# Turning the value product of an attention stage round, and scaling its output instead of its probabilities

## The reference

```python
def block(args):                       # one block of 128 queries of the fox attention
    i, q_b, cq_b = args
    s = jnp.einsum('bqhd,bkhd->bhqk', q_b, k, preferred_element_type=jnp.float32) * (d ** -0.5)
    s = s + cq_b[..., :, None] - ck[:, :, None, :]
    qpos = i * BLOCK_Q + jnp.arange(BLOCK_Q)
    s = jnp.where(kpos[None, :] <= qpos[:, None], s, NEG_INF)
    w = jax.nn.softmax(s, axis=-1).astype(v.dtype)
    return jnp.einsum('bhqk,bkhd->bqhd', w, v)
```

## Time and profile before

| | us |
|---|---|
| time, median of 3 runs | 2120.86 |
| lowest and highest of the 3 | 2119.37, 2122.98 |
| span of the profiled execution, its first to its last instruction | 2126.5 |
| first attention stage: first score product to first output-projection matmul | 134.2 to 243.1 |
| second attention stage, the same | 882.2 to 1015.6 |

### The profile page before, as it was taken

The page is one execution under the profiler, slowest core; times in us unless marked ns, Lnnn a source line. Parts: engine busy times, 40 slices in busy tenths (PEclk is TensorE's granted clock), DMA queues, the critical chain, the costliest instruction groups (busy, mean ns, idle before and its releaser), DMA issues.

```text
span 2126.5 us, 24646 instructions
## 1 busy us (share of the span) xinstructions
PE 1994.8 (94%) x9028; PEld 1647.9 (77%) x9028; DVE 915.8 (43%) x1321; ACT 317.2 (15%) x612; POOL 1240.5 (58%) x719
## 2 busy tenths in 40 slices
PE   7988889999997999999999999988898999999998
PEld 6767778888886787787778888876687778888886
DVE  2469464234338511278263253357537951000234
ACT  0036330000003100056110000020321121000001
POOL 4575356667775455633466667755454365666675
PEclk9989899999999899889999999999998999999999
DMA  5310123333232222211233333332221123333322
GB/s 202 119 40 1 55 72 115 95 99 99 93 95 93 68 88 89 70 35 45 80 100 98 99 96 92 98 109 67 74 81 59 48 82 93 95 99 99 93 95 79
DMA packets 53404, 181.23 MB, mean 85 GB/s; under 512 B 6552, under 2 KB 9290, under 8 KB 53210
## 3 DMA queue, kind: packets, MB, share of 16 engines
q1 hardware_dynamic: 46512, 165.17, 24.6%
q10 hardware_dynamic: 6826, 15.11, 2.1%
HBM read 176.56 MB, written 3.70 MB: 85 GB/s over the span
## 4 chain that ended last, share of the span: by engine, by line
PE 81%; DVE 12%; ACT 2%; issue 2%; POOL 2%; ACTq 0%; POOLq 0%; DVEq 0%
PE PS L577 78%; PE PS L721 2%; DVE PB L1252 1%; DVE X L1360 1%; PE PS L770 1%; DVE PTL L1258 1%; ACT PTH L1750 1%; DVE X L1361 1%; POOL WL L482 1%; DVE X L1322 1%; DVE STL L1594 1%; POOL WH L479 1%; DVE X L1422 0%; DVE XTL L1351 0%; DVE X L1305 0%
## 5 line engine op out<-in xcount | busy, mean ns | idle before, releaser
L479 POOL TENSOR_SCALAR WH<-RW 128x1024 fp32r<-128x1024 f32 x303 | 358.8, 1184 | 742.8 <-PE PS L577 706.1
L482 POOL TENSOR_TENSOR WL<-RW,WH 128x1024 fp32r<-128x1024 f32 x303 | 770.1, 2542 | 25.3
L577 PE MATMUL PS<-XTH,WH 128*128 128x512 f32 x1168 | 464.4, 398 | 15.1 <-ACT HT L1801 11.8
L577 PE MATMUL PS<-XTL,WH 128*128 128x512 f32 x1168 | 461.0, 395 | 0.0
L577 PE MATMUL PS<-XTH,WL 128*128 128x512 f32 x1168 | 460.8, 395 | 0.0
L577 PEld LDWEIGHTS PS<-XTH,WH 128*128 128x128 f32 x1168 | 223.6, 191 | 64.9 <-ACT HT L1801 13.2
L577 PE MATMUL PS<-WL,HSH 128*128 128x512 f32 x688 | 267.6, 390 | 2.1 <-POOL WL L482 2.1
L577 PE MATMUL PS<-WH,HSL 128*128 128x512 f32 x688 | 267.7, 389 | 0.0
L577 PE MATMUL PS<-WH,HSH 128*128 128x512 f32 x688 | 267.6, 389 | 0.0
L577 PEld LDWEIGHTS PS<-XTH,WL 128*128 128x128 f32 x1168 | 223.1, 191 | 47.7
L577 PEld LDWEIGHTS PS<-XTL,WH 128*128 128x128 f32 x1168 | 223.7, 192 | 45.5
(11 more groups left out here) (314 smaller groups left out, 2357.5 us busy)
## 6 DMA issues: line engine op xcount, KB each, us to landing
RW<-stream SPq DMA_DIRECT2D x303, 512.0 KB, 3.5
BC<-gate_rows SPq DMA_DIRECT2D x16, 256.0 KB, 3.2
G<-gain_rows ACTq DMA_DIRECT2D x5, 512.0 KB, 3.6
XS<-xt ACTq DMA_DIRECT2D x4, 512.0 KB, 8.0
X<-x ACTq DMA_DIRECT2D x1, 2048.0 KB, 11.7
G<-bias_vecs ACTq DMA_DIRECT2D x4, 512.0 KB, 5.1
out<-X SPq DMA_DIRECT2D x4, 512.0 KB, 2.6
bias_rows<-QM ACTq DMA_DIRECT2D x1, 1536.0 KB, 7.0
```

What stands on the lines that cost most here:

```text
L479: pool.tensor_scalar(WH[:, j % WS, :], RW[:, j % RAW, :], 1.0, 1.0, ALU.mult, ALU.mult).then_inc(hi_split, 1)
L482: pool.tensor_tensor(WL[:, j % WS, :], RW[:, j % RAW, :], WH[:, j % WS, :].bitcast(F32), ALU.subtract).then_inc(lo_split, 1)
L577: return pe.matmul(o, a, b, start=start, stop=stop)
```

## The change

Softmax probabilities stay unscaled: `sums`, `normalise` and `normalise_last` go. The value product has the transposed probabilities as its stationary operand, one 128x128 block at a time, and streams the values of one head, 64 columns of high and 64 of low part side by side in the new tile `AV`: one matmul of 128 columns for each `PTH` block, one of 64 columns for each `PTL` block. Its output has tokens on partitions. ACT copies the part from the low values (`out_part`), DVE takes the reciprocal, adds the two parts into `OB` and multiplies by the reciprocal into `ON` (`out_normed`). For each pair of heads PE transposes `ON` back (`turn_out`, four transposes), and `out_hi` and `out_lo` split 128x512 once per pair. PE's order in a step becomes turn of head s, scores of head s+2, `turn_out` of a pair in every other step, value product of head s-1. The loop over the fox heads is written out.

```diff
-            def turn(h, r):
+            def turn(h):
                 window = kind_of(h) == "swa"
-                pe.wait_ge(normed, h + 1 + 4 * r)
-                if not window:
-                    pe.wait_ge(last_normed, (h + 1 if h < MLA_H else h + 1 - SWA_H) + 4 * r)
+                pe.wait_ge(expd, 4 * (h + 1))
                 if h:
-                    pe.wait_ge(pt_lo, h + 4 * r)
+                    pe.wait_ge(pt_lo, h)
...
-            def pv(h, r):
+            def pv(h):
...
+                if h >= 2:
+                    pe.wait_ge(o_normed, h - 1)
+                if h % 2 and h >= 3:
+                    pe.wait_ge(o_lo, (h - 1) // 2)
+                for i in range(T):
+                    k0 = max(0, i - 1) if window else 0
+                    for kb in range(k0, i + 1):
+                        p = slice(to[kb] + P * (i - kb), to[kb] + P * (i - kb + 1))
+                        mm(PS[:, bank, i * P:(i + 1) * P], PTH[:, e, p], AV[:, v, kb, e, :], kb == k0, False)
+                    for kb in range(k0, i + 1):
+                        p = slice(to[kb] + P * (i - kb), to[kb] + P * (i - kb + 1))
+                        x = mm(PS[:, bank, i * P:i * P + HD], PTL[:, e, p], AV[:, v, kb, e, 0:HD], False, kb == i)
                 x.then_inc(o_ready, 1)
...
+            def turn_out(p):
+
+                pe.wait_ge(o_normed, 2 * p + 2)
+                for i in range(T):
+                    x = pe.transpose(PS[:, 7, i * P:(i + 1) * P], ON[:, i, :], IDENT[:, :])
+                x.then_inc(o_turned, 1)
+
+            def attend(h0):
+                qk(h0)
+                qk(h0 + 1)
+                for s in range(17):
+                    if s < 16:
+                        turn(h0 + s)
+                    if s + 2 < 16:
+                        qk(h0 + s + 2)
+                    if s % 2 and s >= 3:
+                        turn_out((h0 + s - 3) // 2)
+                    if s:
+                        pv(h0 + s - 1)
...
+            def outward(c, pairs):
+
+                xt = [(XTH[:, k, :], XTL[:, k, :]) for k in range(KD)]
+                pe.wait_ge(o_lo, pairs - 7)
+                chunk(c)
+                wide_tile(0, c, *xt[0], True, False)
+                turn_out(pairs - 1)
+                wide_tile(1, c, *xt[0], True, False)
+                wide_tile(2, c, *xt[0], True, False)
+                pe.wait_ge(o_lo, pairs)
+                wide_tile(3, c, *xt[0], True, False).then_inc(chunk_used, 1)
...
+            def out_normed(h):
+                e, s = h % 2, h % 4
+                ve.wait_ge(expd, 4 * (h + 1))
+                if kind_of(h) == "swa":
+                    ve.wait_ge(sunk, h - 7)
+                    own(ve.tensor_tensor(SM[:, s, :], SM[:, s, :], ES[:, s, :], A))
+                own.mark(ve.reciprocal(SM[:, s, :], SM[:, s, :]))
+                ve.wait_ge(o_part, h + 1)
+                o = PS[:, 6 + e, :].rearrange("p (t n) -> p t n", t=T)[:, :, 0:HD]
+                own(ve.tensor_tensor(OB[:, :, :], o, OB[:, :, :], A))
+                ve.tensor_tensor(ON[:, :, HD * e:HD * (e + 1)], OB[:, :, :], spread(SM[:, s, :], HD, 2),
+                                 M).then_inc(o_normed, 1)
...
+            def out_part(h):
+                act.wait_ge(o_ready, h + 1)
+                if h:
+                    act.wait_ge(o_normed, h)
+                o = PS[:, 6 + h % 2, :].rearrange("p (t n) -> p t n", t=T)[:, :, HD:]
+                act.copy(OB[:, :, :], o).then_inc(o_part, 1)
```

More of the change, by code:

```diff
@@ L538, in _ @@
             stage_values(0, VF[:, :, 0:P])
[L540 to L570, removed]
+            for h in range(FOX0, FOX0 + FOX_H, 2):
+                n = (h - FOX0) // 2
+                if n < 7:
+                    if n:
+                        pool.wait_ge(scored, 4 * h)
+                    stage_pair((n + 1) % 2, QF[:, n + 1, :], KF[:, n + 1, :])
+                if n:
+                    pool.wait_ge(o_ready, h - 2)
+                    stage_values(n % 2, VF[:, :, n * P:(n + 1) * P])
             over_chunks(pool, FIRST["out1"] + WS - 1, CHUNKS, cut)
@@ L931, in _ @@
             pe.wait_ge(plain_out, 4)
[L932 to L935, removed]
+            attend(0)
             def block_end(b, name_out, name_up, name_down, groups, g0, k_tiles, k0):
[L938 removed]
+                outward(FIRST[name_out], 8 if b == 0 else 16)
                 boundary(b)
@@ L995, in _ @@
             pe.wait_ge(evac, E_FOX - 1)
[L996 to L999, removed]
-            with pe.Fori(0, 3) as r:
-                for h in range(FOX0 + 2, FOX0 + 6):
-                    attend_step(h, r, FOX0 + 15)
-            for h in (FOX0 + 14, FOX0 + 15):
-                attend_step(h, 0, FOX0 + 15)
+            attend(FOX0)
             block_end(3, "out1", "up1", "down1", 8, 8, 32, 32)
@@ L1227, in mask @@
                         other = BC[:, h % 2, 0:n]
-                    ve.wait_ge(scored, 4 * h + in_bank + 16 * r)
-                    if kind == "fox":
-                        own.stand()
+                    ve.wait_ge(scored, 4 * h + in_bank)
                     x = ve.tensor_tensor_reduce(out=probs(h)[:, at:at + n], in0=PS[:, bank, col:col + n],
@@ L1255, in probs_lo, with exp_bias @@
-            def probs_lo(h, r):
+            def exp_bias(h):
+                s = h % 4
+                ve.wait_ge(masked, 4 * (h + 1))
+                cq = CTOK[:, :, h - FOX0:h - FOX0 + 1]
+                nb, mn = (v[:, s, :].unsqueeze(2) for v in (NB, MN))
+                own(ve.tensor_tensor(nb, mn, cq, SUB))
+                ve.tensor_tensor(nb, nb, cq, A).then_inc(biased, 1)
+            def probs_lo(h):
                 n = 896 if kind_of(h) == "swa" else 1280
-                ve.wait_ge(pt_hi, h + 1 + 4 * r)
+                ve.wait_ge(pt_hi, h + 1)
@@ new lines, in out_lo, with attend @@
+            def out_lo(p):
+                ve.wait_ge(o_hi, p + 1)
+                ve.tensor_tensor(XTL[:, p % 8, :], PS[:, 7, :], XTH[:, p % 8, :].bitcast(F32),
+                                 SUB).then_inc(o_lo, 1)
+            def attend(h0):
+                for h in (h0, h0 + 1):
+                    mask(h)
+                    if h0:
+                        exp_bias(h)
+                for s in range(19):
+                    if s % 2 == 0 and s >= 4:
+                        out_lo((h0 + s - 4) // 2)
+                    if 2 <= s < 18:
+                        out_normed(h0 + s - 2)
+                    if s + 2 < 16:
+                        mask(h0 + s + 2)
+                        if h0:
+                            exp_bias(h0 + s + 2)
+                    if s < 16:
+                        probs_lo(h0 + s)
@@ new lines, in out_hi, with attend @@
+            def out_hi(p):
+                act.wait_ge(o_turned, p + 1)
+                act.copy(XTH[:, p % 8, :], PS[:, 7, :]).then_inc(o_hi, 1)
+            def attend(h0):
+                exps(h0)
+                exps(h0 + 1)
+                for s in range(18):
+                    if s >= 2:
+                        out_part(h0 + s - 2)
+                    if s < 16:
+                        probs_hi(h0 + s)
+                    if s + 2 < 16:
+                        exps(h0 + s + 2)
+                    if s % 2 and s >= 3:
+                        out_hi((h0 + s - 3) // 2)
```

220 lines of the change are left out of this document (41 added, 179 removed).

## The result

The changed kernel takes 2212.76 us (median of 4 runs, 2201.32 to 2213.55) against 2121.28 us: 1.0407 times as long, 95% interval 1.0385 to 1.0429. The forecast was 2203 us.

What follows compares the result with a forecast made beforehand. PE bounds the fox heads, and its clock decides: low clock there adds 73.7 us, the first stage 5, the projections 3, sum 82, taking the span from 2126.5 to about 2208 and the median to 2203 us; 8 in 10 range 2160 to 2228.

Steps and rivals of the forecast that it cites:

- A: The forecast case: low clock from the fox stage's first scores to its end, 2203 us; chance 0.80.
- the rivals' clocks: Fox stage clock as before (2126 us, 0.06), half at each level (2160, 0.07), or full from second head (2094, 0.07).
- The term of the value product: Both stages: each matmul costs its stationary load, so twenty take 2.2 us at full clock and 4.26 at half.
- The fox stage, 73.7 us forecast: Second attention stage: scores, turns, value products and `turn_out` at half clock sum to 195.0 us, ending 73.7 us later.
- The first stage, 5 us forecast: MLA and SWA heads: -7 and +8 for MLA, +4 for SWA half at each clock level; together +5 us.
- the argument of the fox stage: Scores now follow the turn and the value product keeps loading blocks, so nothing raises the clock; whole stage stays low.
- Projection and loop: Projections behind both stages start at half clock, about 1.5 us each, +3; writing out the fox loop counts 0.
- VectorE's relief: Scaling removed from DVE: worth nothing in the fox stage; in MLA at full clock 5.8 us a head against 6.3.
- The forecast's best case for that stage: First stage with all heads at full clock: -14 us, the lower end of its range.

Runs made afterwards that it cites:

- e2: The changed kernel with the low matmuls (PTL) of the value product streaming 128 columns in place of 64; 2172.0 us, ratio 1.0242 to the kernel before.
- e1: The changed kernel with PE's order in a step again scores first, then turn, no instruction added or removed; 2154.1 us, ratio 1.0161 to the kernel before.
- e3: The changed kernel with both edits, scores first and 128-column low products; 2150.3 us, ratio 1.0136 to the kernel before.
- b1: The kernel before with the scaling of the probabilities left out on VectorE and ScalarE; 2100.3 us, ratio 0.9882.
- e6: e3 plus four overwritten 512-column matmuls on the head's own data ahead of each fox head's value product; 2137.1 us, ratio 1.0071 to the kernel before.
- e8: e3 plus four overwritten 512-column matmuls, identity by identity, ahead of each fox head's value product; 2135.6 us, ratio 1.0064 to the kernel before.
- e5: First stage of e2 joined to the fox heads of the kernel before, written out; 2126.0 us, ratio 1.0001 to the kernel before.
- b2: The kernel before with the loop over fox heads written out on every engine, nothing else; 2126.4 us, ratio 1.0008.

## Why the prediction came out

**The forecast case was right.** Every sign of A is there: clock 0.50 in some 189 of the 201.8 us of the fox stage (48.0, 136.0 and some 5 of the last 11.7; 0.53 in the mean), PE busy in 198.0 of them, VectorE's load 84.6 / 201.8 = 0.42. None of the rivals' clocks is near it.

**The number is closer than its parts.** The forecast for the span was 2208 us, and it is 2211.0. The fox stage was put 5.3 us too high and the first stage 8.0 too low, and that these cancel is luck. The median is 10 us off and not 3, since the profiled execution before was 5.6 us longer than its median: the forecast took that off the changed kernel's span too, whose execution lies at its median.

**The term of the value product was right.** Twenty loads of a stationary block take 4.27 us a head at half clock (4.26 forecast) and 2.23 at full (2.2; 164.84 to 167.07): ten matmuls of 64 streamed columns and ten of 128 take the time of twenty of 128 (4.31 us in e2). The Trainium skill's rule, which would have made the stage 34 us shorter ("TensorE: Matmul & The Clock Gate", section "LDWEIGHTS (loading the stationary operand)"), agrees with this trace at full clock only: at half clock the step is 0.21 us.

**The fox stage, 73.7 us forecast, 68.4 measured.** A head takes 13.03 us by the forecast's terms (6.05 + 2.29 + 4.26 + 0.43) and 13.0 in the profile (967.59 to 993.62 for two). What differs lies at the ends: the first turn comes at 907.76, 10.9 us behind the stage's start and not 12.1, and the clock is up from 947.5 to 951.0 and again at the end, where no scores are left:

```profile
1087.00:1098.70 11.70, 10.93 (x77) 10.76 (x76) 5.42 (x10) 3.69 (x5) 0.00 (x0) 0.79 0.01 1
```

**The first stage, 5 us forecast, 13.0 measured: the term that was mis-sized.** The prices were right, the number of heads at each was not. The MLA heads are 5.6 us at full clock (5.8 forecast) and 10.2 at half (10.4). An SWA head at half clock takes 61.6 / 8 = 7.7 us (7.5 forecast). I had half of the SWA heads at full clock; none is. From 193.9 us on PE is busy 61.60 of 61.60 us at 0.50, and these eight heads take 61.6 us against 43.8, +17.8; the turn of head 0 comes 4.8 us earlier in the stage (141.25), and the MLA heads between come out level. I did not carry the argument of the fox stage over to SWA. But that argument is no rule either: the MLA heads have their scores behind the turn too and ran at 1.00 for 27 us. What sets the three kinds of head apart was not tried.

**The cause: right in its direction, too sharp in its form.** The forecast had it that turn plus wide value product raise the clock, scores do not, and that the change takes both parts away. It does not part the two, it turns their order round, and e1 shows that the old order with the narrow product raises the clock in most heads. The order is worth 2.5 points and the width 1.7, and together 2.7. Neither brings the fox stage back: e3 is at 0.64, the kernel before at 0.83. Besides the width, e3 differs from the kernel before by the missing scaling (b1 stands at 0.82 without it), by the value product's new form and by `turn_out`. No run takes the last two apart, so which of them keeps the clock down is not shown. e6 and e8 show that four wide matmuls ahead of the value product go with a clock of 0.81 and 0.82.

**Projection and loop.** +3 forecast, 3.7 measured for all that lies between and behind the stages, of which no run takes the two projections by themselves; 0 forecast for the loop, 1.0008 measured.

**VectorE's relief** was put at nothing in the fox stage (b1: 2 us) and at some 0.5 us a head in MLA. b1 puts an upper bound on it that is higher: 24 us, 23 of them in the first stage and 14 of those waits. The forecast's best case for that stage, all at full clock, was 14.

## What to carry to other kernels

Multiply each stage's length by its mean granted clock before you compare two kernels: if the products agree while the lengths don't, look at the clock first, and then price the changed operation at both levels of the clock, since not everything doubles. A rewrite that streams fewer columns behind as many stationary blocks or more saves nothing on TensorE and can cost the clock. The order of the same operations can be worth more than their number (2.5 points here), and the profile's busy share shows nothing of it. Profile more than one execution where the clock moves: e2's differ by 20 us. When a change has two parts, run each by itself: here the scaling held the kernel up by 24 us, and half of that was to be had by moving one block of it in MLA and two in SWA to another engine.

## What was unexpected of the hardware

- TensorE at 136.00 busy of 136.00 us was granted half clock for all of them. The Trainium skill ("TensorE: Matmul & The Clock Gate", section "What's actually happening") has activity release the throttle. In this trace being busy in the profile's sense was not enough for it.
- Added matmuls made a kernel faster: e6 and e8 by 0.65 and 0.7 points against e3. The operands' values did not matter (2137.1 and 2135.6 us).
- The same code ran at different clocks: the old fox stage at 0.79 in e5 and 0.87 in b2 (139.5 and 128.5 us), the same operations at 1.00 and then 0.50 within e3's fox stage, and one and the same kernel, e2, in 2156.6 us with a mean clock of 0.944 and in 2171.5 to 2176.3 with 0.934 to 0.935. What sets that was not tried and stays open.
